# Sample-group attention scores: four key pages side by side on partitions, queries laid block-diagonally, the softmax bias added by VectorE

## The reference, cut to what matters

```python
MOBA_BLOCK = 256; MOBA_TOPK = 3; PAGE_SIZE = 128; PAST_LEN = 1024
k_mean = jnp.mean(kb.astype(jnp.float32), axis=2)            # one mean key per block of 256
gate = jnp.einsum('hqd,hnd->hqn', qh.astype(jnp.float32), k_mean)
gate = jnp.where(fully_past[None], gate, -jnp.inf)
_, top = lax.top_k(gate, n_top)                              # 3 of the 4 past blocks
...
s = jnp.einsum('hqd,hqskd->hqsk', qh, kg, preferred_element_type=jnp.float32) * scale
s = s - slopes[:, None, None, None] * (qpos - key_pos).astype(jnp.float32)
s = jnp.where(valid, s, -jnp.inf)
pr = jax.nn.softmax(s.reshape(ATT_HEADS, qc, -1), axis=-1).reshape(s.shape)
return jnp.einsum('hqsk,hqskd->hqd', pr.astype(vg.dtype), vg)
```

## Time and profile before

| | |
|---|---|
| median of 3 runs (lowest, highest) | 1308.75 us (1308.27, 1309.34) |
| profiled execution | 1308.36 us |
| its span | 1306.7 us |
| mean granted clock of PE | 0.998 of full |
| PE, DVE, ACT, POOL busy | 1296.9, 764.6, 650.2, 232.7 us |
| key scores, L1698, 1536 records | 32.1 us |
| value product, L1736 | 144 groups of four tiles |

### The profile page before, as it was taken

The page is one execution under the profiler, slowest core; times in us unless marked ns, Lnnn a source line. Parts: engine busy times, 40 slices in busy tenths (PEclk is TensorE's granted clock), DMA queues, the critical chain, the costliest instruction groups (busy, mean ns, idle before and its releaser), DMA issues.

```text
span 1306.7 us, 27046 instructions
## 1 busy us (share of the span) xinstructions
PE 1296.9 (99%) x10969; PEld 1253.0 (96%) x10969; DVE 764.6 (59%) x787; ACT 650.2 (50%) x734; POOL 232.7 (18%) x372
## 2 busy tenths in 40 slices
PE   9999999999999999999999999999999999999998
PEld 7999999999879999999999999999998799999998
DVE  5555555677676655644555555565866675555433
ACT  6555543435463655553365555333446456555433
POOL 1020000357541000000101000012865220000010
PEclk9999999999999999999999999999999999999999
DMA  6665444658895444444445554446589844444442
GB/s 196 201 211 185 161 139 151 208 177 227 262 350 170 133 161 145 144 153 145 153 156 183 183 174 132 149 149 215 168 254 321 284 129 161 160 133 157 145 149 68
DMA packets 211423, 233.18 MB, mean 178 GB/s; under 512 B 14974, under 2 KB 205192, under 8 KB 211348
## 3 DMA queue, kind: packets, MB, share of 16 engines
q1 hardware_dynamic: 203388, 209.10, 50.1%
q0 software_dynamic: 7840, 23.01, 5.3%
q10 hardware_dynamic: 120, 0.03, 0.0%
HBM read 226.90 MB, written 5.32 MB: 178 GB/s over the span
## 4 chain that ended last, share of the span: by engine, by line
PE 96%; DMA 1%; DVE 1%; SPq 1%; issue 0%; ACT 0%; ACTq 0%; DVEq 0%
PE ps L1427 24%; PE ps L1429 24%; PE ps L1428 24%; PE ps L1547 4%; PE ps L1549 4%; PE ps L1548 4%; PE ps L1698 2%; PE ps L1736 2%; DMA kbuf<-in_cache_k 1%; PE ps L1875 1%; PE ps L1877 1%; PE ps L1876 1%; PE ps L1716 1%; PE ps L1588 1%; SPq L403 0%; DMA g_rows<-in_pool_scale 0%
## 5 line engine op out<-in xcount | busy, mean ns | idle before, releaser
L695 ACT ACTIVATE w_hi<-w_raw 128x2048 fp32r<-128x2048 f32 x167 | 319.8, 1915 | 521.6 <-PE ps L1429 418.5
L1007 DVE TENSOR_TENSOR w_lo<-w_raw,w_hi 128x2048 fp32r<-128x2048 f32 x159 | 366.1, 2303 | 194.4 <-ACT w_hi L695 190.0
L1427 PE MATMUL ps<-h_hi,w_hi 128*128 128x320 f32 x768 | 237.9, 310 | 0.7 <-DVE h_lo L1093 0.7
L1429 PE MATMUL ps<-h_hi,w_lo 128*128 128x320 f32 x768 | 237.3, 309 | 0.0
L1428 PE MATMUL ps<-h_lo,w_hi 128*128 128x320 f32 x768 | 237.3, 309 | 0.0
L1427 PE MATMUL ps<-g_hi,w_hi 128*128 128x320 f32 x704 | 218.0, 310 | 0.0
L1429 PE MATMUL ps<-g_hi,w_lo 128*128 128x320 f32 x704 | 217.5, 309 | 0.0
L1428 PE MATMUL ps<-g_lo,w_hi 128*128 128x320 f32 x704 | 217.5, 309 | 0.0
L1427 PE MATMUL ps<-act_hi,w_hi 128*128 128x320 f32 x704 | 216.5, 308 | 0.0
L1428 PE MATMUL ps<-act_lo,w_hi 128*128 128x320 f32 x704 | 216.5, 308 | 0.0
L1429 PE MATMUL ps<-act_hi,w_lo 128*128 128x320 f32 x704 | 216.5, 308 | 0.0
(11 more groups left out here) (295 smaller groups left out, 1734.0 us busy)
## 6 DMA issues: line engine op xcount, KB each, us to landing
w_raw<-in_ffn_w_in SPq DMA_DIRECT2D x87, 1024.0 KB, 5.1
w_raw<-in_ffn_w_out SPq DMA_DIRECT2D x32, 896.0 KB, 4.8
w_raw<-in_w_in SPq DMA_DIRECT2D x22, 1024.0 KB, 5.5
kbuf<-in_cache_k SPq DMA_DIRECT2D x96, 192.0 KB, 3.2
w_raw<-in_ffn_w_out SPq DMA_DIRECT2D x16, 1024.0 KB, 5.2
w_raw<-in_w_out SPq DMA_DIRECT2D x8, 1024.0 KB, 7.1
kbuf<-in_cache_k POOLq DMA_DIRECT2D x32, 192.0 KB, 3.0
kbuf<-in_cache_v SPq DMA_DIRECT2D x32, 192.0 KB, 4.3
```

The lines of the kernel that those rows point to most:

```text
L695: act.activation(w_hi[:, slot, :], w_raw[:, slot, :], ACT.Copy).then_inc(hi_done, 1)
L1007: dve.tensor_tensor(w_lo[:, slot, :], w_raw[:, slot, :], w_hi[:, slot, :].bitcast(F32), ALU.subtract).then_inc(split_done, 1)
L1427: pe.matmul(out, w_hi[:, slot, w], hi[:, k, :], start=(k == 0), stop=False)
L1429: ins = pe.matmul(out, w_lo[:, slot, w], hi[:, k, :], start=False, stop=(k == k_all - 1))
```

## The change

- Key pages are loaded with four pages side by side: page j of a half goes to partitions 32j to 32j + 31, four consecutive tokens in a row of 6 KB (load_k, first_k). After the 32x32 turn partition 32a + d' has dimension d' of page a.
- qprep lays the queries out block-diagonally: on the partitions of page a the 8 query columns 8a to 8a + 7 are filled, the others zero. So a product with all 128 rows and 32 columns gives four pages times 8 queries. key_scores has 24 products instead of 96 a pair, own_scores 12 instead of 8; a row is now (sequence, head group, page, query), and the three heads lie behind one another in columns, 288 for each (256 past, 32 own).
- A softmax row's parts now lie on four rows: DVE gathers them by 32x32 transposes of small tiles (blk, bias_s), works out which block falls out, and adds the bias itself over all scores; ACT has three exponentials without bias. soft_sum sums over the rows in the same way.
- transpose_probs has six transposes of 128 columns and three of 32 or 64; probs_evac has eight copies instead of three.
- The padding of PE's instructions is gone, and the constants are laid out anew (one more, own_head).

The diff, without constants, buffers and the renumbered columns of ss; of the three softmax helpers only the new lines, since the old ones stand above:

```diff
-        sp_e.dma_start(kbuf[home][:, 4 * half + j, :],
-                       A["cache_k"][L, page[j]].rearrange("t h d -> t (h d)")).then_inc(k_landed[home][half], 16)
+        sp_e.dma_start(kbuf[home][32 * j:32 * j + 32, 4 * half:4 * half + 4, :],
+                       A["cache_k"][L, page[j]].rearrange("(t r) h d -> t r (h d)", r=4)).then_inc(k_landed[home][half], 16)
...
 def qprep(L, p):
     pool.drain()
-    for bb in range(2):
-        for gg in range(2):
-            at_g = 384 * bb + 192 * gg
-            dst = q_sc[p][:, at_g:at_g + 216].rearrange("p (s x) -> p s x", s=3)[:, :, 0:64]
-            ins = pool.tensor_copy(dst.rearrange("p s (j c) -> p s j c", j=2)[:, :, :, 0:8],
-                                   q_rep[:, 3 * gg:3 * gg + 3, :, p * 16 + 8 * bb:p * 16 + 8 * bb + 8])
+    for a in range(4):
+        r = slice(32 * a, 32 * a + 32)
+        for bb in range(2):
+            dst = q_sc[p][r, 384 * bb:384 * bb + 384].rearrange("p (x c) -> p x c", c=32)[:, :, 8 * a:8 * a + 8]
+            src = q_rep[r, :, :, p * 16 + 8 * bb:p * 16 + 8 * bb + 8].rearrange("p h j q -> p (h j) q")
+            ins = pool.tensor_copy(dst, src)
     ins.then_inc(qp_ok, 1)
     pool.drain()
     for half in range(2):
         r = slice(HD * half, HD * half + HD)
-        own = q_bd[r, 0:192].rearrange("p (b x) -> p b x", b=2)
-        for f in range(3):
-            ins = pool.tensor_copy(own[:, :, 8 * half + 40 * f:8 * half + 40 * f + 8],
-                                   q_smp[r, f, p * 16:p * 16 + 16].rearrange("p (b q) -> p b q", b=2))
+        own = q_bd[r, :].rearrange("p (f x) -> p f x", f=3)[:, :, 40 * half:40 * half + 40]
+        for bb in range(2):
+            ins = pool.tensor_copy(own[:, :, 32 * bb:32 * bb + 8],
+                                   q_smp[r, :, p * 16 + 8 * bb:p * 16 + 8 * bb + 8])
     ins.then_inc(qb_ok, 1)
...
-def exps(p, parts=range(5)):
+def exps(p, parts=range(3)):
     if 0 in parts:
         act.wait_ge(sm_bias, L * 4 + p + 1)
     for n in parts:
-        a, b = (256 * n, 256 * n + 256) if n < 4 else (PAST_LEN, PAST_LEN + SMP)
-        ins = act.activation(sp[p][:, a:b], sp[p][:, a:b], ACT.Exp, bias=ss[:, 32 + n:33 + n],
-                             accum_out=ss[:, 40 + n:41 + n])
-    if 4 in parts:
+        part = sp[p][:, 288 * n:288 * n + 288]
+        ins = act.activation(part, part, ACT.Exp, accum_out=blk[:, n:n + 1])
+    if 2 in parts:
         ins.then_inc(sm_exp, 1)
 def probs_evac(p):
     pt = pt_s[p % 2]
-    used = lambda r, part, a: ps[r, t_bank(p, part), a:512].rearrange("p (n x) -> p n x", x=32)[:, :, 0:24]
-    to = lambda r, a, b: pt[r, a:b].rearrange("p (n x) -> p n x", x=24)
-    every, own = slice(0, P), slice(0, SMP)
-    act.wait_ge(pt2_done, L * 8 + p * 2 + 1)
-    act.activation(to(every, 0, 384), used(every, 0, 0), ACT.Copy).then_inc(pt2_evac, 1)
-    act.wait_ge(pt2_done, L * 8 + p * 2 + 2)
-    act.activation(to(every, 384, 768), used(every, 1, 0), ACT.Copy)
-    act.activation(to(own, 768, 864), used(own, 2, 384), ACT.Copy).then_inc(pt2_evac, 1)
+    w = slice(32 * (p // 2), 32 * (p // 2) + 32)
+    for n in range(3):
+        if n != 1:
+            act.wait_ge(pt2_done, L * 8 + p * 2 + 1 + n // 2)
+        for quad in range(2):
+            at = 256 * (n % 2) + P * quad
+            past = ps[:, t_bank(p, n // 2), at:at + P].rearrange("p (g a q) -> p g a q", g=4, a=4)
+            to = pt[:, 384 * quad:384 * quad + 384].rearrange("p (a g n q) -> p g a n q", a=4, g=4, n=3)[:, :, :, n, :]
+            ins = act.activation(to, past, ACT.Copy)
+        if n == 1:
+            ins.then_inc(pt2_evac, 1)
+    for bb in range(2):
+        own = ps[w, t_bank(p, 2), P:].rearrange("p (n b g x) -> p n b g x", n=3, b=2, g=2)[:, :, bb, :, 24 * bb:24 * bb + 8]
+        to = pt[w, 768:864].rearrange("p (b g n q) -> p n b g q", b=2, g=2, n=3)[:, :, bb, :, :]
+        ins = act.activation(to, own, ACT.Copy)
+    ins.then_inc(pt2_evac, 1)
...
+def block_rows(a, b):
+    return blk[:, 32 * a:32 * b].rearrange("p (c e q) -> p c e q", e=2, q=NT)
+def past_blocks(first):
+    return blk[:, 32 * first:32 * first + 64].rearrange("p (k x) -> p x k", k=2)[:, 0:3, :]
 def soft_in(p):
...
     dve.wait_ge(own_done, L * 4 + p + 1)
...
+    raw = ps[:, 2:4, :].rearrange("p b n -> p (b n)")
+    dve.tensor_reduce(past_blocks(0), raw[:, 0:768].rearrange("p (n k x) -> p n k x", n=3, k=2), AX, ALU.add)
+    probs = sp[p][:, 0:864].rearrange("p (n x) -> p n x", n=3)
+    for n in range(3):
+        dve.tensor_tensor(probs[:, n, 0:256].rearrange("p (k t r) -> p k r t", k=2, r=4),
+                          raw[:, 256 * n:256 * n + 256].rearrange("p (k r t) -> p k r t", k=2, r=4),
+                          cst["alibi_s"][:, 256 * n:256 * n + 256].rearrange("p (k r t) -> p k r t", k=2, r=4), ALU.add)
+    dve.tensor_tensor(probs[:, :, 256:288], raw[:, 768:864].rearrange("p (n x) -> p n x", n=3),
+                      cst["alibi_own"][:, p, :].rearrange("p (n x) -> p n x", n=3), ALU.add).then_inc(sm_in, 1)
+    dve.drain()
+    dve.tensor_reduce(past_blocks(2), probs[:, :, 0:256].rearrange("p n (k x) -> p n k x", k=2), AX, ALU.max)
+    dve.tensor_reduce(blk[:, 128:131], probs[:, :, 256:288], AX, ALU.max)
     dve.drain()
 def soft_bias(p):
...
+    each = lambda t, n: t.unsqueeze(1).to_broadcast([P, n, NT])
+    w = ss[:, 0:32].rearrange("p (c q) -> p c q", q=NT)
+    least, last, top = ss[:, 32:40], ss[:, 40:48], ss[:, 48:56]
+    peak = ss[:, 56:96].rearrange("p (c q) -> p c q", q=NT)
+    dve.transpose(blk[:], blk[:])
+    dve.drain()
+    sums, peaks = block_rows(0, 2), block_rows(2, 4)
+    dve.tensor_tensor(w, sums[:, :, 0, :], sums[:, :, 1, :], ALU.add)
+    dve.tensor_tensor(peak[:, 0:4, :], peaks[:, :, 0, :], peaks[:, :, 1, :], ALU.max)
+    dve.tensor_reduce(peak[:, 4, :], blk[:, 128:160].rearrange("p (a q) -> p q a", a=4), AX, ALU.max)
+    dve.drain()
+    dve.tensor_reduce(least, w.rearrange("p c q -> p q c"), AX, ALU.min)
+    dve.drain()
+    dve.tensor_tensor(w, w, each(least, 4), ALU.is_le)
+    dve.drain()
+    dve.tensor_tensor(w, w, cst["rank"][:].unsqueeze(2).to_broadcast([P, 4, NT]), ALU.mult)
+    dve.drain()
+    dve.tensor_reduce(last, w.rearrange("p c q -> p q c"), AX, ALU.max)
+    dve.drain()
+    dve.tensor_tensor(w, w, each(last, 4), ALU.is_equal)
+    dve.drain()
+    dve.scalar_tensor_tensor(out=peak[:, 0:4, :], in0=w, scalar=-BIG, in1=peak[:, 0:4, :], op0=ALU.mult, op1=ALU.add)
+    dve.drain()
+    dve.tensor_reduce(top, peak.rearrange("p c q -> p q c"), AX, ALU.max)
+    dve.drain()
+    for e in range(2):
+        dve.scalar_tensor_tensor(out=bias_s[:, 0:64].rearrange("p (c e q) -> p c e q", e=2, q=NT)[:, :, e, :],
+                                 in0=w, scalar=-BIG, in1=each(top, 4), op0=ALU.mult, op1=ALU.subtract)
+    dve.tensor_scalar(bias_s[:, 64:96].rearrange("p (a q) -> p a q", q=NT), each(top, 4), -1.0, None, ALU.mult)
+    dve.drain()
+    dve.transpose(bias_s[:], bias_s[:])
+    dve.drain()
+    probs = sp[p][:, 0:864].rearrange("p (n x) -> p n x", n=3)
+    past, own = probs[:, :, 0:256].rearrange("p n (k x) -> p n k x", k=2), probs[:, :, 256:288]
+    past_bias = bias_s[:, 0:64].rearrange("p (k x) -> p x k", k=2)[:, 0:3, :].unsqueeze(3).to_broadcast([P, 3, 2, P])
+    dve.tensor_tensor(past, past, past_bias, ALU.add)
+    dve.tensor_tensor(own, own, bias_s[:, 64:67].unsqueeze(2).to_broadcast([P, 3, 32]), ALU.add).then_inc(sm_bias, 1)
 def soft_sum(p):
     dve.wait_ge(sm_exp, L * 4 + p + 1)
...
+    dve.transpose(blk[:, 0:32], blk[:, 0:32])
+    dve.drain()
+    dve.tensor_reduce(ss[:, 32:40], blk[:, 0:32].rearrange("p (k q) -> p q k", q=NT), AX, ALU.add)
+    dve.drain()
+    dve.tensor_tensor(ss[:, 0:32].rearrange("p (n q) -> p n q", q=NT), ss[:, 32:40].unsqueeze(1).to_broadcast([P, 4, NT]),
+                      cst["own_head"][:].unsqueeze(2).to_broadcast([P, 4, NT]), ALU.mult)
+    dve.drain()
+    dve.transpose(ss[:, 0:32], ss[:, 0:32])
+    dve.drain()
+    dve.tensor_reduce(ss[:, 96:97], ss[:, 0:3], AX, ALU.add)
+    dve.drain()
+    dve.reciprocal(ss[:, 98 + p:99 + p], ss[:, 96:97]).then_inc(rs_ok, 1)
...
-FETCH = {2: 99, 5: 0, 10: 244}
+FETCH = {}
...
-def key_scores(p, parts=range(6)):
-
-    if 0 in parts:
-        pe.wait_ge(kt_ok, L * 16 + p * 4 + 4)
-    for n in parts:
-        slot, j = divmod(n, 2)
-        for g in range(4):
-            c = (3 * (g % 2) + slot) * HD + 32 * j
-            at_q = 192 * g + 64 * slot + 32 * j
-            for r in range(4):
-                R = slice(32 * r, 32 * r + 32)
-                ins = pe.matmul(ps[32 * g:32 * g + 32, 2 + r, 0:256], q_sc[p][R, at_q:at_q + 32],
-                                kbuf[k_home(p, g // 2)][R, :, c:c + 32], start=(n == 0), stop=(n == 5))
-    if 5 in parts:
-        ins.then_inc(sc_done, 1)
+def key_scores(p):
+    pe.wait_ge(kt_ok, L * 16 + p * 4 + 4)
+    for n in range(3):
+        for j in range(2):
+            for g in range(4):
```

(43 more changed lines are left out.)

54 lines of the change are left out of this document (22 added, 32 removed).

## The result

| | before | after |
|---|---|---|
| median (range) | 1308.88 us (1308.27 to 1309.34) | 1327.24 us (1321.63 to 1329.4) |
| ratio, 95% interval | | 1.0134 [1.0102, 1.0166] |
| profiled execution, its span | 1308.36, 1306.7 us | 1329.4, 1326.9 us |

What follows compares the result with a forecast made beforehand. TensorE (PE) was taken to bound the kernel, busy 99%. Its 9.2 us saving is lost to waits for VectorE, leaving +0.7 us a layer, 1.4 in all: 1309.8, plus 0.4 for the median, 1310.2 us; range 1304 to 1317.

Steps and rivals of the forecast that it cites:

- Part 1: TensorE's scores: key scores from 3.95 to 2.6 us, own scores 0.18 more; net 1.15 us less a pair, 9.2 over eight.
- rival 4: TensorE's tiles don't overlap with their loads: key scores stay at 3.95 us, own scores grow; 1318 us, chance 0.04.
- Part 2: VectorE's softmax steps per pair: soft_in 0.55 us less, soft_bias 3.0 more at 4.5, soft_sum 1.05 more.
- rival 2: VectorE's small steps are dear, soft_bias at 5.5 us, every wait grows: slower, 1314 us, chance 0.15.
- Part 3: Three places of each layer where TensorE waits because VectorE ends last; together +0.7 us a layer.
- first place: Before sample_scores(1), TensorE waits some 3.6 us for maxima behind soft_bias(0); start at +2.45 us, mix(6) at +1.3.
- The step that failed: Up to pair 2 VectorE is another 1.05 and 2.45 us later, absorbed by existing waits; pair 2 starts at +1.3.
- The second place: Transposes before sample_scores(3) wait 0.5 us for a VectorE evacuation; pair 3 starts at +0.6, mix(11) at -0.6.
- rival 3: TensorE's clock falls to 1.2 GHz for the pair behind each new wait: 3 us a layer, 1316 us, chance 0.15.
- The key pages: Pages arrive in 6 KB rows on 32 partitions, speed unknown; a landing 2 us later would cost 1 to 2 us.
- The third place: Wait for o_evac(1) before the value tokens: 1.1 us, +0.5; with another 0.2 at the product, +0.7 us a layer.
- The removed alignments: TensorE's instruction stream without padding costs nothing if thinner key scores hide fetches; a stall would show as idle time without releaser.

Runs made afterwards that it cites:

- experiment 3: Changed kernel with GpSimd's subtractions for weight chunks 8 to 11 of each layer's mixing stage cut to 8 columns: 1322.0 us.
- experiment 4: Changed kernel with 24 TensorE products ahead of its wait before the second pair's scores: 1335.5 us; the same with GpSimd's chunk 8 to 11 subtractions cut: 1314.8 us.
- the ninth new placement: Changed kernel's arithmetic with softmax steps reordered, lastly the attention's low parts moved ahead of the bias additions: 1306.4 us against 1308.1, ratio 0.9987.

## Why the prediction was wrong, step by step

- **Part 1 held.** Key scores 2.61 us (2.6 predicted), own scores 0.3 (0.54); rival 4, with loads that don't overlap, had 3.95.
- **Part 2 held, on a free machine.** soft_in 3.73 (3.3: a 256-column addition takes 0.46 to the next, not 0.33), soft_bias 4.8 to 5.2 (4.5), nearer to the forecast than rival 2's 5.5. With GpSimd quiet VectorE is 27.5 us busier (28 predicted), complete 37.6: the rest is standing still.
- **Part 3, first place: the wait held, what follows it did not.** The wait is 3.96 us (3.6). Behind it mix(6) was to start at +1.3; it starts at 305.70 where before had 302.76, +2.9, because the scores run at half clock. With the wait filled and GpSimd quiet it starts at +1.5.
- **The step that failed: that nothing more is lost between the first place and the third.** The prediction said: "the waits that it had absorb that: I find each evacuation done within some tenths of PE's need." The small steps were costed from rows in which GpSimd subtracted nothing beside them. Beside its subtractions soft_bias had 9.2 and 6.8 us and q_dec 4.2; PE waited 3.0 us for an evacuation and 4.4 for the copy to o_past, a place that the sum doesn't have. The second place itself had 0.8 us, once (0.5 predicted). Taking GpSimd's work away gave back 5.3 us (experiment 3). The row of before at 308.81, a small step of 0.46 instead of 0.23 us, I did not ask about; GpSimd was issuing transfers then, not subtracting, and what held that step up stays open.
- **The larger term that the sum put at nothing is the clock, rival 3.** It stood at 0.15 and 3 us a layer. With GpSimd quiet it was worth 3.6 us a layer at the first place, the keys' wait with it (experiment 4), and the changed kernel has 20.6 us at half clock, since its other long waits have falls of their own.
- **The key pages, "a landing 2 us later would cost 1 to 2 us"**: they land 1.6 us later, and that cost 5.9 us with GpSimd quiet, as the wait is over 2 us and the clock falls behind it. It stood in the text and not in the sum.
- The third place: 1.68 and 1.32 us of wait (1.1 predicted). The removed alignments cost nothing that shows: no idle time of PE without a releaser.

With the collision taken away the kernel is at 1322.0 us, and with the first place's wait filled as well at 1314.8, inside the range. The three lengthen one another: a later VectorE meets GpSimd, the longer wait drops the clock. So the 5.3, 7.2 and 5.9 us can't be added up: the last two both hold the keys' wait. I added the costs one by one and gave each its chance as if only one could come.

## What to carry to other kernels

Before small steps are moved to VectorE, list what GpSimd does at these times: beside GpSimd's subtractions here an operation with two SBUF inputs stood until one of GpSimd's instructions ended, so a step of 0.2 us cost up to 1.3, and once 5. Count a wait of PE of some 3 us with the half clock that can follow it, and keep such costs in the sum, not beside it. A gain on the engine that bounds is worth what the others can follow: here 9.2 us of TensorE came to 1.6 us, in the ninth new placement, and 1.6 us are little more than the noise.
